# A hybrid attention and convolution block on one core: the convolution input gated before its transposes

## The reference, cut to what matters

```python
h = rmsnorm(x, g_mix[l])
proj = h @ w_in[l]
u = proj[..., c_v:c_u] + b_glu[l]          # 1024 columns, b_glu is a vector of 1024
gate_a = jax.nn.sigmoid(proj[..., c_u:c_ga])
gate_c = jax.nn.sigmoid(proj[..., c_ga:])
# conformer_conv(u, ...):
a, g = jnp.split(u, 2, axis=-1)            # 512 values, 512 gates
z = a * jax.nn.sigmoid(g)
z = depthwise_conv(z, w_dw)  + b_dw        # 31 taps over time, causal, one filter a channel
z = layernorm(z, ln_g, ln_b)
return jax.nn.silu(z)
```

## Time and profile before

| | |
|---|---|
| median of 3 timed runs | 348.99 us |
| time of the profiled execution | 349.28 us |
| span of its trace | 347.5 us |
| PE busy | 341.5 us (98%) |
| DVE busy | 248.7 us (72%) |
| ACT busy | 199.0 us (57%) |
| mean granted TensorE clock | 1.000 of full |

### The profile page before, as it was taken

The page is one execution under the profiler, slowest core; times in us unless marked ns, Lnnn a source line. Parts: engine busy times, 40 slices in busy tenths (PEclk is TensorE's granted clock), DMA queues, the critical chain, the costliest instruction groups (busy, mean ns, idle before and its releaser), DMA issues.

```text
span 347.5 us, 4632 instructions
## 1 busy us (share of the span) xinstructions
PE 341.5 (98%) x1740; PEld 287.3 (83%) x1740; DVE 248.7 (72%) x302; ACT 199.0 (57%) x254; POOL 9.1 (3%) x17
## 2 busy tenths in 40 slices
PE   8999999999999999999999999999999999999994
PEld 5888888888887888888888888888888888889884
DVE  2969999999999799946766747638466394663813
ACT  4995896596987566444874436424355253551534
POOL 1000010100000300000000000000000000000000
PEclk9999999999999999999999999999999999999999
DMA  8999478967164816692537571935719448260003
GB/s 276 351 387 388 158 236 214 297 187 239 32 212 130 283 74 241 197 314 84 193 121 243 191 254 49 338 135 159 256 68 306 177 139 243 101 241 0 0 0 121
DMA packets 35005, 66.33 MB, mean 191 GB/s; under 512 B 1424, under 2 KB 6064, under 8 KB 34992
## 3 DMA queue, kind: packets, MB, share of 16 engines
q1 hardware_dynamic: 34056, 63.56, 53.7%
q0 software_dynamic: 576, 2.10, 3.2%
q10 hardware_dynamic: 360, 0.49, 0.4%
HBM read 63.00 MB, written 1.05 MB: 184 GB/s over the span
## 4 chain that ended last, share of the span: by engine, by line
PE 98%; DVE 0%; issue 0%; DVEq 0%; ACT 0%
PE ps L1074 19%; PE ps L1075 19%; PE ps L1076 19%; PE ps L1350 17%; PE ps L1358 9%; PE ps L1227 4%; PE ps L1068 3%; PE ps L1231 2%; PE ps L1121 2%; PE ps L1132 1%; PE ps L1101 1%; PE ps L1177 1%; PE ps L1196 1%; PE ps L1311 1%; PE ps L1402 0%; PE ps L1401 0%
## 5 line engine op out<-in xcount | busy, mean ns | idle before, releaser
L1074 PE MATMUL ps<-w_hi,a_both 128*128 128x512 f32 x240 | 94.5, 394 | 0.0
L1075 PE MATMUL ps<-w_hi,a_both 128*128 128x512 f32 x240 | 93.5, 390 | 0.0
L1076 PE MATMUL ps<-w_lo,a_both 128*128 128x512 f32 x240 | 93.5, 390 | 0.0
L1009 DVE TENSOR_TENSOR w_lo<-raw,w_hi 128x2048 fp32r<-128x2048 f32 x28 | 63.5, 2287 | 6.2 <-ACT w_hi L696 6.2
L454 ACT CAST w_hi<-raw 128x2048 fp32r<-128x2048 f32 (+1 forms) x30 | 53.9, 1804 | 20.2 <-PE ps L1076 19.7
L1350 PE MATMUL ps<-b_both,w_hi 128*128 128x512 f32 x256 | 61.3, 390 | 0.0
L747 DVE TENSOR_TENSOR w_lo<-raw,w_hi 128x2048 fp32r<-128x2048 f32 x26 | 59.3, 2283 | 1.7 <-ACT w_hi L454 1.7
L696 ACT CAST w_hi<-raw 128x2048 fp32r<-128x2048 f32 x28 | 52.8, 1914 | 7.5 <-PE ps L1076 7.5
L1350 PEld LDWEIGHTS ps<-b_both,w_hi 128*128 128x128 f32 x256 | 47.4, 188 | 9.4
L1076 PEld LDWEIGHTS ps<-w_lo,a_both 128*128 128x128 f32 x240 | 45.0, 188 | 9.5
L1074 PEld LDWEIGHTS ps<-w_hi,a_both 128*128 128x128 f32 x240 | 45.1, 188 | 9.4 <-issue 0.2
(11 more groups left out here) (154 smaller groups left out, 318.2 us busy)
## 6 DMA issues: line engine op xcount, KB each, us to landing
raw<-in_w_ff_dram SPq DMA_DIRECT2D x32, 1024.0 KB, 5.5
raw<-in_w_in_dram SPq DMA_DIRECT2D x14, 1024.0 KB, 6.3
raw<-in_w_out_dram SPq DMA_DIRECT2D x4, 1024.0 KB, 5.1
raw<-in_w_in_dram SPq DMA_DIRECT2D x14, 256.0 KB, 5.6
silu_x<-gates POOLq DMA_DIRECT2D x4, 512.0 KB, 6.1
raw<-in_w_attn_up_dram SPq DMA_DIRECT2D x2, 1024.0 KB, 5.0
raw<-in_w_conv_pw_dram SPq DMA_DIRECT2D x2, 1024.0 KB, 5.0
res<-in_x_dram SPq DMA_DIRECT2D x2, 512.0 KB, 3.9
```

Source lines behind the costliest of these rows:

```text
L1009: nc.vector.tensor_tensor(w_lo[:, slot], raw[:, slot], w_hi[:, slot].bitcast(F32), ALU.subtract).then_inc(lo_made, 1)
L1074: nc.tensor.matmul(dst, lo[:, tok], w_hi[:, slot, k], start=start, stop=False, skip_group_check=seeded)
L1075: nc.tensor.matmul(dst, hi[:, tok], w_hi[:, slot, k], start=False, stop=False, skip_group_check=seeded)
L1076: return nc.tensor.matmul(dst, hi[:, tok], w_lo[:, slot, k], start=False, stop=stop, skip_group_check=seeded)
```

## The change

The bias `b_glu` is no longer part of `vec`; SP loads it to all 128 partitions (512 KB) into a part of `gates` that is free at that time, between the transfers of units 2 and 3. DVE makes the scaled sum (PSUM times `rstd` plus bias) with tokens on partitions, gates first, in four instructions of 128x256; ACT takes the sigmoid in place, one instruction of 128 x 512; DVE multiplies, one instruction of 128x512. PE turns the product alone, 4 transposes a half block instead of 8, after unit 2 for hb 0 and after the third column block of unit 4 for hb 1. ACT copies the turned product to `z` and makes tap 0. `take(0)` and `take(1)` are gone. Four of DVE's 100 convolution products move from steps 2 and 3 to steps 10 to 13.

```diff
+S_GLU = 3
+S_Z = 2
+Z_BANKS = (4, 7)
-CONV_AT = {2: 6, 3: 12, 4: 9, 5: 9, 6: 6, 7: 5, 8: 2, 9: 6, 10: 8, 11: 12, 12: 11, 13: 9, 14: 5}
+CONV_AT = {2: 5, 3: 9, 4: 9, 5: 9, 6: 6, 7: 5, 8: 2, 9: 6, 10: 9, 11: 13, 12: 12, 13: 10, 14: 5}
+        glu_bc = gates[:, 1, 1]
@@ SyncE, between the transfers of unit 2 and of w_dw
+            sp.dma_start(glu_bc, b_glu.to_broadcast([P, D])).then_inc(glu_full, 16)
@@ ScalarE
-            for row, v in ((V_BGLU, b_glu), (V_BDW, b_dw), (V_LNG, ln_g), (V_LNB, ln_b), (V_GFFN, g_ffn)):
+            for row, v in ((V_BDW, b_dw), (V_LNG, ln_g), (V_LNB, ln_b), (V_GFFN, g_ffn)):
+            def gates_sigmoid(hb):
+                act.wait_ge(gates_lin, TT * (hb + 1))
+                part = nat[:, :, hb * W + W // 2:hb * W + W]
+                nc.scalar.activation(part, part, ACT.Sigmoid).then_inc(glu_sig, 1)
+            def z_out(hb):
+                act.wait_ge(z_tr, hb + 1)
+                if hb == 0:
+                    act.wait_ge(const_made, 4)
+                nc.scalar.copy(z[:, 2 * hb:2 * hb + 2, PAD:PAD + T],
+                               ps[:, Z_BANKS[hb]].rearrange("p (c t) -> p c t", c=2)).then_inc(z_made, 1)
+                act.wait_ge(z_made, hb + 1)
+                act.wait_ge(vec_made, 2)
+                for c in (2 * hb, 2 * hb + 1):
+                    nc.scalar.activation(conv[:, c], z[:, c, 0:T], ACT.Identity, scale=dw[:, c:c + 1],
+                                         bias=vec[:, V_BDW + c:V_BDW + c + 1]).then_inc(conv_first, 1)
@@ steps: gates_sigmoid(0) before high(3), gates_sigmoid(1) after high(6),
@@        z_out(0) after high(5), z_out(1) after high(7)
...
@@ VectorE, gated(0) before low_pair(3, ...), gated(1) at the head of step 3
+            def gated(hb):
+                dve.wait_ge(used, 2 * hb + 2)
+                dve.wait_ge(rstd_made, 1)
+                dve.wait_ge(glu_full, 16)
+                for part, made in ((1, gates_lin), (0, values_lin)):
+                    at = part * W // 2
+                    bias = part * C + hb * W // 2
+                    for t in range(TT):
+                        nc.vector.scalar_tensor_tensor(out=nat[:, t, hb * W + at:hb * W + at + W // 2],
+                                                       in0=ps[:, 2 * hb + t, at:at + W // 2], scalar=rstd[:, 0, t:t + 1],
+                                                       in1=glu_bc[:, bias:bias + W // 2], op0=ALU.mult,
+                                                       op1=ALU.add).then_inc(made, 1)
+                dve.wait_ge(values_lin, TT * (hb + 1))
+                dve.wait_ge(glu_sig, hb + 1)
+                values = nat[:, :, hb * W:hb * W + W // 2]
+                nc.vector.tensor_tensor(values, values, nat[:, :, hb * W + W // 2:hb * W + W],
+                                        ALU.mult).then_inc(glu_made, 1)
@@ TensorE, glu_transposed gone; z_transposed(0) after unit 2, z_transposed(1) in unit 4
+            def z_transposed(hb):
+                pe.wait_ge(glu_made, hb + 1)
+                if hb == 1:
+                    pe.wait_ge(vec_made, 2)
+                for c in range(2):
+                    for t in range(TT):
+                        last = transpose(ps[:, Z_BANKS[hb], c * T + t * P:c * T + t * P + P],
+                                         nat[:, t, hb * W + c * P:hb * W + c * P + P])
+                last.then_inc(z_tr, 1)
```

More of the change, by code:

```diff
@@ L46 @@
 S_VEC = 1
-GLU_AT = {2: 0, 4: 1}
+S_GLU = 3
+S_Z = 2
+Z_BANKS = (4, 7)
 Q_BANKS = (0, 1, 4, 5)
@@ L77 @@
 AX = mybir.AxisListType
-V_BGLU, V_BDW, V_LNG, V_LNB, V_GFFN = 0, 8, 12, 16, 20
-VROWS = 28
+V_BDW, V_LNG, V_LNB, V_GFFN = 0, 4, 8, 12
+VROWS = 20
 DW_ROWS = 112
@@ L275, in build @@
         gate_made = sem("gate_made")
-        glu_tr = sem("glu_tr")
+        glu_full = sem("glu_full")
+        gates_lin = sem("gates_lin")
+        values_lin = sem("values_lin")
         glu_sig = sem("glu_sig")
+        glu_made = sem("glu_made")
+        z_tr = sem("z_tr")
         z_made = sem("z_made")
@@ L500, in take @@
                 act.wait_ge(used, 2 * b + 2)
-                if b == 0:
-                    act.wait_ge(rstd_made, 1)
                 if b == GA:
@@ L506, in take @@
                     dst, fn = gates[:, 0, :, 0:W], ACT.Copy
-                elif b < 2:
-                    dst, fn = nat[:, :, b * W:b * W + W], ACT.Copy
                 elif b == V:
@@ L565, in tap_products @@
                 for tap in TAPS_ACT.get(step, ()):
-                    act.wait_ge(z_made, CC)
+                    act.wait_ge(z_made, 2)
                     i = tap - TAPS_DVE
@@ L584, in _ @@
                 if n == S_VEC:
-                    take(0)
                     act.wait_ge(vec_tr, 1)
@@ L589, in _ @@
                     nc.scalar.copy(dw[:], ps[:, SB0 + 1, P:P + TAPS * CC]).then_inc(vec_made, 1)
+                    gates_sigmoid(0)
                     high(AHEAD)
-                if n and n + AHEAD < U_LOOP + AHEAD_LOOP and n not in GLU_AT and n not in S_VALUES and n - 1 not in S_SCORES:
+                if n and n + AHEAD < U_LOOP + AHEAD_LOOP and n not in S_VALUES and n - 1 not in S_SCORES:
                     high(n + AHEAD)
[L593 to L605, removed]
+                if n == S_ROW:
+                    gates_sigmoid(1)
                 if n == U_CONV:
                     set_bias(1)
+                if n == S_Z:
+                    z_out(0)
+                if n == 2 * Q:
+                    z_out(1)
                 tap_products(n)
@@ L615, in _ @@
                     queries_out()
-                elif n < U_ATTN and n % 2 == 1 and 0 < n // 2 <= GA:
+                elif n < U_ATTN and n % 2 == 1 and 2 <= n // 2 <= GA:
                     take(n // 2)
@@ L632, in _ @@
                 if n == S_GATE:
-                    act.wait_ge(evac, GA - 1)
+                    act.wait_ge(evac, GA - 3)
                     part = gates[:, 0, :, 0:W]
@@ L788, in _ @@
             nc.vector.tensor_scalar(ms[:, 0], sq_sum[:, 0, 0:TT], 1.0 / D, EPS, ALU.mult, ALU.add).then_inc(ms_made, 1)
+            def gated(hb):
[15 more added lines that the diff above has]
+                                        ALU.mult).then_inc(glu_made, 1)
+            gated(0)
             dve.wait_ge(fourth_hi, 1)
@@ L798, in conv_products @@
                     if tap == 1:
+                        dve.wait_ge(vec_made, 2)
                         dve.wait_ge(conv_first, c + 1)
@@ L855, in _ @@
             for n in range(U_LOOP):
[L856 to L865, removed]
+                if n == S_GLU:
+                    gated(1)
                 if n == S_QSCALE:
@@ L918, in _ @@
                     dve.wait_ge(used, n + 1)
-                    dve.wait_ge(evac, len(ORDER) - 2)
+                    dve.wait_ge(evac, len(ORDER) - 4)
                     dve.wait_ge(gate_made, 1)
@@ L1111, in _ @@
                         last.then_inc(x_tr, 1)
-            pe.wait_ge(vec_full, 16 * 5)
+            pe.wait_ge(vec_full, 16 * 4)
             pe.wait_ge(gmix_made, 1)
@@ L1202, in pairs_transposed @@
                 probs_transposed(2 * group + 1)
-            def glu_transposed(hb):
-                pe.wait_ge(vec_made, 2)
-                pe.wait_ge(evac, hb + 1)
+            def z_transposed(hb):
+                pe.wait_ge(glu_made, hb + 1)
                 if hb == 1:
[L1208 to L1214, removed]
+                    pe.wait_ge(vec_made, 2)
[4 more added lines that the diff above has]
+                last.then_inc(z_tr, 1)
             def turned(n, banks):
@@ L1220, in turned @@
                     if n == 2 * Q and c == 2:
+                        pe.wait_ge(z_made, 1)
+                    if n == 2 * K and c == 2:
+                        pe.wait_ge(row_made, 1)
+                    if n == 2 * K and c == 3:
                         pe.wait_ge(z_made, 2)
-                    if n == 2 * K and c == 2:
-                        pe.wait_ge(z_made, CC)
                     cols = slice(c * P, c * P + P)
@@ L1232, in turned @@
                                                 start=False, stop=kk == KD - 1)
-                    if n == 2 * Q and c == 1:
-                        glu_transposed(GLU_AT[n])
+                    if n == 2 * Q and c == 2:
+                        z_transposed(1)
                 last.then_inc(used, 1)
@@ L1248, in _ @@
                 if half == 0 and b in (Q, K):
-                    pe.wait_ge(evac, b - 1)
+                    pe.wait_ge(values_lin, TT * (b - 1))
                 if n == 2 * GA:
@@ L1252, in _ @@
                 if half == 0 and b > GA:
-                    pe.wait_ge(evac, b - 3)
+                    pe.wait_ge(evac, b - 5)
                 if n == 2 * V:
@@ L1265, in _ @@
                     unit(n, a_hi, a_lo, HK * half, lambda t: 2 * (b % 2) + t, half == 0, half == 1,
-                         (lambda: glu_transposed(GLU_AT[n])) if n in GLU_AT else
```

(6 more changed lines are left out.)

## The result

The kernel after takes 353.06 us in the median of six runs, the kernel before on the same chips 349.26; the ratio is 1.0101, with an interval of 1.0086 to 1.0117. One of the six, of 1216 us, was disturbed and is not in the ratio; the others lie between 351.18 and 353.77. Measured again later, on one chip, it was 352.00 against 349.14, ratio 1.0084 (1.0070 to 1.0098). The forecast was 349.8, with a range up to 351.3: the direction is right, the size is off by a factor of five.

What follows compares the result with a forecast made beforehand. PE bounds the kernel; it saves 0.86 us but stalls 1.65 us for DVE's convolution, so its transposes load 0.79 us later: 348.99 + 0.79 = 349.78 us, range 348.7 to 351.3.

Steps and rivals of the forecast that it cites:

- What bounds the kernel, and where the change would be decided: PE, busy 341.5 of 347.5 us; decided where PE waits for DVE's convolution, with 0.44 us of slack.
- PE's saving, 0.86 us: Two groups of 4 transposes instead of 8 in units 2 and 4 save PE 0.86 us, give or take 0.07.
- DVE's work, +2.78 us: Sums and products add 4.36 us, 1.58 is removed: net +2.78 us ahead of the convolution's end at 107.67.
- The transfer, 1.3 us, unit 5 at 24.6: The 512 KB bias transfer makes unit 3 and all later units land 1.3 us later, unit 5 at 24.6.
- the third rival: The instruction packet delays unit 5 if still moving when it comes, near 24.8: +2.1, 351.1 us; chance 0.19.
- `low(7)` at 38.83: DVE reaches `low(7)` at 38.83, 0.29 us later than before, with four products (1.58 us) still owed.
- The two stops give 0.34 and 0.33 back, four products are owed: DVE's stops before row maxima and second reciprocal shrink, leaving it 0.38 early; owed products make +1.20 from step 14.
- `conv_made` at 110.10: DVE's last convolution instruction ends at 110.10 instead of 108.90, 1.20 us later.
- The second `glu_made` has a slack of 1.3: In unit 4 the second product is ready at 33.1, PE wants it at 34.4: slack 1.3 us, no wait.
- The sum, a stall of 1.65: PE, ready at 108.48, stalls 1.65 us before the convolution's transposes and loads 0.79 later: 349.78 against the median.

Runs made afterwards that it cites:

- a6: Kernel after, convolution transposes moved to the end of unit 16, second product transposes behind unit 4's fourth column block: 349.00 us, ratio 0.9992.
- b5: Kernel before with 4 transposes a half block instead of 8, gates left out of the result: 348.64 us, ratio 0.9984.
- a3: Kernel after without the bias transfer, GpSimd filling those 512 KB with zeros instead: 350.39 us, ratio 1.0040.
- a1: Kernel after with 12 bf16 matmuls of zeros on PE ahead of its wait for the convolution: 351.44 us, ratio 1.0066.
- d1: Kernel after once more, unchanged, on one chip: 352.00 us, ratio 1.0084; its six times make two groups.
- b1: Kernel before with the 512 KB bias transfer added, read by nothing: 349.29 us, ratio 1.0003.
- b3: Kernel before with the bias transfer and seven more DVE instructions, the first four behind the transfer: 350.31 us, ratio 1.0036.

## Why the prediction was right or wrong, point by point

- *What bounds the kernel, and where the change would be decided*: right. PE stalls ahead of the transposes of the convolution, released by DVE.
- *PE's saving, 0.86 us*: right. Units 2 and 3 give 0.41, unit 4 in a6 0.41, and b5 is 0.66 lower by its median.
- *DVE's work, +2.78 us*: right. Four sums 1.66, product 0.69, `low(6)` 0.61 behind it, as sized.
- *The transfer, 1.3 us, unit 5 at 24.6*: **the step that failed first.** Unit 5 landed at 26.25, 1.65 later. The transfer costs 1.4 to 1.5 (a3 against a1), so 0.1 to 0.2 more than its term. The instruction packet, which the forecast left to the third rival, costs 0.65: it starts at 22.38, and units 4 and 5 land 3.35 apart instead of 2.7. The other 0.8 or 0.9 stood ahead of the transfer: the last piece of unit 2, issued before it, lands at 15.63, in the kernel before at 14.71. This part changes from execution to execution. In d1, the same kernel, that piece lands at 14.77, unit 4 at 22.07 as forecast within 0.2, the packet costs 1.0 and unit 5 lands at 25.76; PE runs 0.45 earlier there too, and its idle time at unit 16 is 2.65 again. So the forecast lacked three things at unit 5: the packet (0.65 to 1.0 us), 0.1 to 0.2 of the transfer, and loads that start 0.5 to 0.9 later against PE than in the trace of before, for which no run shows a reason. The rival had the packet near 24.8, from the count of slower matmuls. That was wrong: in every kernel with the new code it comes at 21.5 to 22.4, in every one with the old code at 23.7 to 24.5. Its condition, unit 5 still moving, was wrong as well: that held in b1 and b3, and unit 5 came on time. It does not need the transfer either; in a3 units 4 and 5 are 3.3 apart without it. Why the packet moved is open.
- *`low(7)` at 38.83*: 40.47, later by 1.64, like unit 5.
- *The two stops give 0.34 and 0.33 back, four products are owed*: right. DVE is 1.93 us later than before at `low(7)`, 1.58 at L850 and 1.22 at the reciprocal, and 1.22 + 1.58 = 2.80.
- *`conv_made` at 110.10*: 112.08. 2.80 behind the old 108.90 would be 111.70. The missing 0.38 is the gap of 0.48 ahead of the addition, which is 0.10 in the trace of before.
- *The second `glu_made` has a slack of 1.3*: it had none; PE lost 0.54 there, again unit 5.
- *The sum, a stall of 1.65*: 2.81. And I priced only the waiting, at full clock. A long stall can have a second price: 1.35 us in the profiled run, shown by a1 and borne out by the two groups of d1. The prediction did not have this term at all. Nor did it have the 0.2 us at the end of the span.

The third rival's 351.1 us is what the kernel takes at full clock within 0.6 us (351.7 in d1); I gave it 0.19. It named the right packet and the right unit, but its time for the packet and its condition were both wrong, so part of that nearness is luck.

*The Trainium skill, "TensorE: Matmul & The Clock Gate", section "What's actually happening", says that the default state of TensorE's clock is throttled and activity releases it. The rows agree with it: 0.64 behind 2.65 us of idling, 1.00 with zeros multiplied in the same place. Had the rule been weighed in the prediction, the stall would have had this risk beside it, which the forecast's range left out; no run here shows a fall in a stall as short as the 1.65 us that was forecast.*

## What to carry to other kernels

Where the busiest engine has no idle time, what it saves is worth no more than the slack of the engines it waits for, and what their own stops give back when it comes earlier. Here that was 0.44 us, 90 us behind the edit, and 0.53 us of stops, enough for b5's 0.66, but not once work and late inputs were added. Find the tightest hand-over downstream and move it before cutting the busy engine's work. Idle time early in another engine's order is no reserve if the same change also makes its inputs late: the two costs were hidden one by one and not together. One long stall of TensorE can cost more than the same waiting in pieces, since the clock may fall in it. And a transfer in a full queue can do more than shift the ones behind it: look which other packets come in at that time, and which unit they hit.

## What the runs showed of the hardware that was not expected

- Within an idle stretch of 2.65 us TensorE's granted clock fell, and the next 4 us had a mean of 0.64; in the one profile each with waits of 2.25, 1.2 and 0.7 us it stayed at 1.00. By their mean clocks, about half of the executions of the kernel after did not fall. With 12 bf16 matmuls of zeros in the stall none of four did.
- The 16 KB instruction packet on one of 16 DMA engines moved from 23.7 to 22.4 us with the new code, and one 1 MB transfer landed 0.65 us late (0.3 to 1.5 over all traces). It is not the one that lands within 0.83 us of the packet's start, but the one behind it.
- With the transfer of 512 KB early in the kernel 0.61 us lie between the last landing of the output and the end of the span, in all twelve traces that have it, and 0.38 in the five that don't.
- A gap of 0.48 us on VectorE appears and goes with the instructions ahead of it: it is there at the 192nd entry of the trace, and 0.10 or none at the 191st and the 194th.
